# A streaming encoder's MoE layers: 16 KB read-back, zeros during the mixer, down loads on ACT's queue

## The reference

```python
def moe_layer(x, router_w, router_b, w_gate, w_up, w_down, sh_gate, sh_up, sh_down):
    ...
    _, idx = lax.top_k(masked, TOP_K)                    # 8 of 64 experts
    wts = jnp.take_along_axis(scores, idx, axis=1)
    wts = wts / jnp.sum(wts, axis=-1, keepdims=True) * ROUTED_SCALE
    routed = routed_experts(x2, idx, wts, w_gate, w_up, w_down)
    shared = (jax.nn.silu(x2 @ sh_gate) * (x2 @ sh_up)) @ sh_down
    return (routed.astype(x.dtype) + shared).reshape(B, S, D)
# routed_experts, for each block of tokens of one expert e:
        hb = jax.nn.silu(xb @ w_gate[e]) * (xb @ w_up[e])
        acc = acc.at[toks].add((hb @ w_down[e]).astype(jnp.float32) * gates[:, None])
```

## Time and profile before

| | |
|---|---|
| median of 3 runs | 1355.86 us (1353.26 to 1357.22) |
| the profiled execution, its own time | 1357.68 us |
| its span in the profile | 1355.5 us |
| PE busy | 1285.6 us (95%) |
| DVE, ACT, POOL busy | 568.3, 337.3, 270.5 us |
| moved by DMA | 445.95 MB, of them 428.13 by the hardware queue q1 |
| mean granted TensorE clock | 0.977 of full speed |

### The profile page before, as it was taken

The page is one execution under the profiler, slowest core; times in us unless marked ns, Lnnn a source line. Parts: engine busy times, 40 slices in busy tenths (PEclk is TensorE's granted clock), DMA queues, the critical chain, the costliest instruction groups (busy, mean ns, idle before and its releaser), DMA issues.

```text
span 1355.5 us, 17904 instructions
## 1 busy us (share of the span) xinstructions
PE 1285.6 (95%) x6318; PEld 648.6 (48%) x6318; DVE 568.3 (42%) x1229; ACT 337.3 (25%) x689; POOL 270.5 (20%) x233
## 2 busy tenths in 40 slices
PE   6999999999999999999989789999999999999985
PEld 4566546545444454444533565544444444444432
DVE  0665556433333343333342784332333333343336
ACT  0643412222222222222211341222222212222113
POOL 6110102122211121121202202121122211221120
PEclk9999898999999999999998889999999999999988
DMA  9403028699999999999999725999999999999992
GB/s 279 128 7 125 11 99 327 264 387 414 408 390 420 420 391 421 420 420 392 419 323 413 301 94 189 378 406 417 381 420 420 420 395 419 420 390 419 374 353 86
DMA packets 82323, 445.95 MB, mean 329 GB/s; under 512 B 20626, under 2 KB 22786, under 8 KB 32224
## 3 DMA queue, kind: packets, MB, share of 16 engines
q1 hardware_dynamic: 69248, 428.13, 79.2%
q0 software_dynamic: 13024, 17.13, 4.1%
HBM read 436.37 MB, written 35.31 MB: 348 GB/s over the span
## 4 chain that ended last, share of the span: by engine, by line
PE 88%; DMA 6%; DVE 3%; ACT 2%; issue 1%; SPq 0%; DVEq 0%
PE bank L975 32%; PE bank L894 19%; PE bank L928 15%; PE bank L922 8%; DMA sb_wslot<-in_moe_w_up_dram 4%; PE bank L878 3%; PE bank L1317 3%; PE bank L1103 1%; PE bank L1066 1%; DMA sb_wslot<-in_pool_scale_dram 1%; PE bank L987 1%; DMA sb_x<-in_x_sample_dram 1%; PE bank L1094 0%; PE bank L1234 0%; ACT sb_xt L1504 0%
## 5 line engine op out<-in xcount | busy, mean ns | idle before, releaser
L757 POOL TENSOR_TENSOR sb_sent<-sb_yh,sb_yl 128x1024 f32<-128x1024 f32 x56 | 135.5, 2420 | 651.9 <-DVE sb_yl L1729 579.0
L975 PE MATMUL bank<-sb_wslot,sb_xt 128*64 128x512 f32 x1024 | 232.1, 607 | 12.0 <-DMA sb_wslot<-in_moe_w_up_dram 12.0
L928 PE MATMUL bank<-sb_wslot,sb_ht 128*64 128x512 f32 x1024 | 231.0, 593 | 0.0
L975 PE MATMUL bank<-sb_wslot,sb_xg_own 128*64 128x512 f32 x1024 | 226.5, 595 | 1.7 <-ACT sb_xg_own L1448 1.7
L1723 DVE TENSOR_TENSOR sb_x<-sb_x,bank 128x512 f32<-128x512 f32 (+1 forms) x284 | 175.5, 680 | 80.4 <-PE bank L922 80.1
L1748 DVE TENSOR_TENSOR sb_hh<-sb_sg,bank 128x256 f32<-128x256 f32 x64 | 27.0, 421 | 399.4 <-ACT sb_sg L1473 399.4
L1729 DVE SCALAR_TENSOR_TENSOR sb_yl<-bank,sb_gslot,sb_yh 128x512 fp32r<-128x512 f32 x128 | 96.1, 750 | 160.6 <-ACT sb_yh L1455 160.6
L1473 ACT ACTIVATE sb_sg<-bank 128x256 f32<-128x256 f32 x64 | 24.6, 384 | 533.0 <-PE bank L975 533.0
L975 PEld LDWEIGHTS bank<-sb_wslot,sb_xt 128*64 128x64 f32 x1024 | 71.8, 139 | 156.0 <-issue 156.0
L894 PE MATMUL bank<-sb_pick,sb_xh 128*128 128x512 f32 x384 | 144.2, 405 | 0.0
L928 PEld LDWEIGHTS bank<-sb_wslot,sb_ht 128*64 128x64 f32 x1024 | 72.8, 137 | 144.6 <-issue 140.7
(11 more groups left out here) (325 smaller groups left out, 1149.3 us busy)
## 6 DMA issues: line engine op xcount, KB each, us to landing
sb_wslot<-in_moe_w_gate_dram SPq DMA_DIRECT2D x64, 2048.0 KB, 10.5
sb_wslot<-in_moe_w_up_dram SPq DMA_DIRECT2D x64, 2048.0 KB, 15.4
sb_wslot<-in_moe_w_down_dram SPq DMA_DIRECT2D x64, 2048.0 KB, 17.5
sb_w_in_hi<-in_w_in_dram SPq DMA_DIRECT2D x2, 2048.0 KB, 15.0
sb_w_in_lo<-in_w_out_dram SPq DMA_DIRECT2D x1, 4096.0 KB, 13.9
tail_slots<-sb_sent POOLq DMA_DIRECT2D x8, 512.0 KB, 10.8
sb_w_in_lo<-in_w_in_dram SPq DMA_DIRECT2D x2, 1024.0 KB, 11.1
sb_ln_g<-in_ln_g_dram POOLq DMA_DIRECT2D x4, 512.0 KB, 4.9
```

Source lines behind the costliest of these rows:

```text
L757: gp.tensor_tensor(sent[:, :], yh[:, :].bitcast(F32), yl[:, :].bitcast(F32), ALU.add).then_inc(s["sent_made"], 1)
L928: last = pe.matmul(y_b[c][64 * e:64 * e + 64, :], ht[:, k, 64 * e:64 * e + 64], w_down[u][:, e, k * D + c * 512:k * D + (c + 1) * 512], st ...
L975: last = pe.matmul(gu_b[64 * e:64 * e + 64, :], xgt[b][:, k, sl], w_gu[u][:, :, e, k * FE:(k + 1) * FE], start=k == 0, stop=k == DK_SLICES ...
```

## The change

Four things are done. (1) `slots_zeroed` becomes one semaphore for both layers; POOL sets `sq` to zero after the stores of ckv and krope and from it writes both layers' `tail_slots` with 16 DMAs of 128 runs of 2 KB (256 KB each), issued before it waits for `qh`. POOL's experts part waits for them before the first send, and DVE's first `square_sums` waits too. The memset of `sent` and its four DMAs behind the routing are gone. (2) The read-back takes half h of a token's eight slots (4096 values, 16 KB in one run) instead of 512 columns of all eight slots (8 runs of 2 KB). Partitions 0 to 63 then hold slots 0 to 3 and partitions 64 to 127 slots 4 to 7, all columns. Two adds of 2048 and 1024 values, a move of 64 x 1024 values and a third add of 64 x 1024 sum them. (3) SP no longer loads the down weights in its loop. ACT issues the down load of pair i + 1 in turn i, behind `high_out` of pair i - 1 (which has waited for that pair's down), and at the end of a body that of the next but one, behind the second `high_out`. The first down loads of a layer and those of further rounds stay on SP. (4) Where SP waited for `down_done` it now goes on with the next gate and up.

```diff
@@ -70,6 +70,7 @@
 DIRECT = P + WT_COLS
 TAIL_SLOTS = 64 * TOPK
 NOWHERE = 2.0 * TAIL_SLOTS
+ZERO_PARTS = DEPTH * TAIL_SLOTS * D // (P * 512)
 SLOTS = 64
 ZEROED = 13
 MIX_PARAMS = 10
@@ -556,6 +557,7 @@
         state_in = sem("state_in")
         w_out_in = sem("w_out_in")
         zeroed = sem("zeroed")
+        slots_zeroed = sem("slots_zeroed")
         wg2_zeroed = sem("wg2_zeroed")
         q_lev_zeroed = sem("q_lev_zeroed")
         k_lev_zeroed = sem("k_lev_zeroed")
@@ -599,7 +601,7 @@
             "gu_done0", "gu_done1", "down_done0", "down_done1", "xg_done0", "xg_done1", "xg_copied0", "xg_copied1",
             "pick_ready", "sg_ready", "h_ready", "ht_done", "ht_copied", "place_done", "place_copied", "gate_ready",
             "yh_ready0", "yh_ready1", "sum_done", "added", "y_half", "y_ready", "next_round",
-            "y_summed", "tail_sent", "slot_free", "sent_made", "slots_zeroed", "tail_in", "tail_step")} for l in range(DEPTH)]
+            "y_summed", "tail_sent", "slot_free", "sent_made", "tail_in", "tail_step")} for l in range(DEPTH)]
         for n in ("pool_in", "pool_c_in", "pool_scaled"):
             L[1][n] = sem(n)
 
@@ -647,27 +649,21 @@
             with sp.Fori(1, TURNS - 1) as j:
                 sp.wait_ge(s["gu_done1"], j)
                 load_pair(sp, l, 1, 2 * j + 1, GU)
-                sp.wait_ge(s["down_done0"], j)
-                load_pair(sp, l, 0, 2 * j, DN)
                 sp.wait_ge(s["gu_done0"], j + 1)
                 load_pair(sp, l, 0, 2 * j + 2, GU)
-                sp.wait_ge(s["down_done1"], j)
-                load_pair(sp, l, 1, 2 * j + 1, DN)
             sp.wait_ge(s["gu_done1"], TURNS - 1)
             load_pair(sp, l, 1, PAIRS - 1, GU)
-            for u in range(2):
-                sp.wait_ge(s[f"down_done{u}"], TURNS - 1)
-                load_pair(sp, l, u, PAIRS - 2 + u, DN)
             sp.wait_ge(s["rounds_ready"], 1)
             rounds = sp.value_load(n_rounds[0:1, 0:1], min_val=1, max_val=MAX_ROUNDS)
             with sp.If(rounds - 1):
                 with sp.Fori(1, rounds) as r:
+                    for u in range(2):
+                        sp.wait_ge(s[f"down_done{u}"], r * TURNS)
+                        load_pair(sp, l, u, u, DN)
                     with sp.Fori(0, TURNS) as j:
                         for u in range(2):
                             sp.wait_ge(s[f"gu_done{u}"], r * TURNS + j)
                             load_pair(sp, l, u, 2 * j + u, GU)
-                            sp.wait_ge(s[f"down_done{u}"], r * TURNS + j)
-                            load_pair(sp, l, u, 2 * j + u, DN)
             if l == 0:
                 uses = rounds * TURNS
                 sp.wait_ge(s["gu_done0"], uses)
@@ -743,11 +739,7 @@
             rounds = gp.value_load(n_rounds[0:1, 0:1], min_val=1, max_val=MAX_ROUNDS)
             banks.full(gp, ("lgT", l))
             gp.wait_ge(s["init"], 5 - l)
-            gp.memset(sent[:, :], 0.0).then_inc(s["sent_made"], 1)
-            gp.wait_ge(s["sent_made"], 1)
-            for k in range(TAIL_SLOTS // P):
-                gp.dma_start(slots[k * P:(k + 1) * P, :], sent[:, :]).then_inc(s["slots_zeroed"], 16)
-            gp.wait_ge(s["slots_zeroed"], 16 * (TAIL_SLOTS // P))
+            gp.wait_ge(slots_zeroed, 16 * ZERO_PARTS)
             gp.wait_ge(s["w_ready"], 2 - l)
 
             def send(r, turn, u):
@@ -755,7 +747,7 @@
                 i = r * PAIRS + turn
                 gp.wait_ge(s["y_ready"], 2 * i + 1)
                 gp.tensor_tensor(sent[:, :], yh[:, :].bitcast(F32), yl[:, :].bitcast(F32), ALU.add).then_inc(s["sent_made"], 1)
-                gp.wait_ge(s["sent_made"], r * SENT + turn + 2)
+                gp.wait_ge(s["sent_made"], r * SENT + turn + 1)
                 gp.sem_inc(s["y_summed"], 1)
                 gp.indirect_dma_start(out=slots, out_offset=bass.IndirectOffsetOnAxis(ap=slot_at[1 - u][:, 0:1], axis=0),
                                       in_=sent[:, :], in_offset=None, bounds_check=TAIL_SLOTS - 1, oob_is_err=False)\
@@ -767,17 +759,18 @@
                 with gp.Fori(0, SENT // 2) as j:
                     for u in range(2):
                         send(r, 2 * j + u, u)
-            src = slots.rearrange("(t k) d -> t k d", k=TOPK)
-            for c in range(2):
+            src = slots.rearrange("(t k) d -> t (k d)", k=TOPK)
+            for h in range(2):
                 for r0, n in ((0, TAIL), (SAMPLE_ROW, N_DEC)):
-                    gp.dma_start(xg_own[64 * c + r0:64 * c + r0 + n, :].rearrange("p (k d) -> p k d", k=TOPK),
-                                 src[r0:r0 + n, :, c * 512:(c + 1) * 512]).then_inc(s["tail_in"], 16)
+                    gp.dma_start(xg_own[64 * h + r0:64 * h + r0 + n, :], src[r0:r0 + n, h * 4096:(h + 1) * 4096]).then_inc(s["tail_in"], 16)
             gp.wait_ge(s["tail_in"], 16 * 4)
-            for i, w in enumerate((2048, 1024, 512)):
+            for i, w in enumerate((2048, 1024)):
                 gp.tensor_tensor(xg_own[:, 0:w], xg_own[:, 0:w], xg_own[:, w:2 * w], ALU.add).then_inc(s["tail_step"], 1)
                 gp.wait_ge(s["tail_step"], i + 1)
-            gp.dma_start(xg_own[0:64, 512:1024], xg_own[64:128, 0:512]).then_inc(s["tail_in"], 16)
+            gp.dma_start(xg_own[0:64, 1024:2048], xg_own[64:128, 0:1024]).then_inc(s["tail_in"], 16)
             gp.wait_ge(s["tail_in"], 16 * 5)
+            gp.tensor_tensor(xg_own[0:64, 0:1024], xg_own[0:64, 0:1024], xg_own[0:64, 1024:2048], ALU.add).then_inc(s["tail_step"], 1)
+            gp.wait_ge(s["tail_step"], 3)
             gp.wait_ge(s["added"], rounds * ROUND_ADDS + 1)
             gp.tensor_tensor(x[0:64, 2, :], x[0:64, 2, :], xg_own[0:64, 0:1024], ALU.add).then_inc(s["tail_step"], 1)
 
@@ -835,6 +828,12 @@
                 gp.dma_start(po[0:2 * P, :].rearrange("(t p) c -> p t c", p=P), src[:, 0:2, :]).then_inc(stored, 16)
                 gp.dma_start(po[2 * P:N_PROMPT, :], src[0:TAIL, 2, :]).then_inc(stored, 16)
                 gp.dma_start(so, src[SAMPLE_ROW:SAMPLE_ROW + N_DEC, 2, :]).then_inc(stored, 16)
+            gp.memset(sq[:, :], 0.0).then_inc(zeroed, 1)
+            gp.wait_ge(zeroed, ZEROED + 1)
+            for l in range(DEPTH):
+                rows = a["tail_slots"][l].rearrange("(p r) d -> p (r d)", p=P)
+                for c0 in range(0, rows.shape[1], 512):
+                    gp.dma_start(rows[:, c0:c0 + 512], sq[:, :]).then_inc(slots_zeroed, 16)
             banks.full(gp, ("qh", MH - 1))
             gp.memset(q_few_rot, 0.0).then_inc(few_zeroed, 1)
             for j in range(2):
@@ -1473,6 +1472,8 @@
                     act.activation(sg[:, :], gu_b[:, 0:FE], ACT.Silu).then_inc(s["sg_ready"], 1)
                     if m:
                         high_out(1 - u, i - 1, n - 1 + u, summed)
+                        if not last_body or m < BODY - 1:
+                            load_pair(act, l, 1 - u, BODY * j + (m + 1), DN)
                         hidden_out(i)
                     act.wait_ge(s["place_done"], i + 2)
                     nt = TILES if places_tail(m, last_body) else 2
@@ -1486,6 +1487,8 @@
                         hidden_out(i)
                     if m == BODY - 1:
                         high_out(u, i, n, summed if last_body else summed + 1)
+                        if not last_body:
+                            load_pair(act, l, u, BODY * j + (BODY + 1), DN)
 
             with act.Fori(0, rounds) as r:
                 for kk in range(DK_SLICES):
@@ -1936,6 +1939,8 @@
             turn_queries(range(4, 8))
 
             def square_sums(t):
+                if t == 0:
+                    dve.wait_ge(slots_zeroed, 16 * ZERO_PARTS)
                 for c, j in CHUNK_PARTS[4 * t:4 * t + 4]:
                     banks.copied(dve, ("o", c, j))
                 o, q = og[:, 2 * t:2 * t + 2, :, :].rearrange("p c j n -> p (c j) n"), sq[:, :].rearrange("p (i n) -> p i n", i=4)
```

## The result

The changed kernel took 1370.24 us (median of 4 runs, 1366.79 to 1373.23), the kernel before 1354.91 us beside it (1353.26 to 1357.22). The ratio is 1.0107, with a 95% interval of 1.0086 to 1.0128. It is 15 us slower, outside the predicted range of 1339 to 1364. The profiled span grew from 1355.5 to 1369.9 us, by 14.4.

What follows compares the result with a forecast made beforehand. It took TensorE, busy 95% of the span, as the bound, with DMA only 0.45 us a turn from it. Layer 1's +2.2 us and layer 0's +0.4 made +2.6 us, so 1358 us, range 1339 to 1364.

Steps and rivals of the forecast that it cites:

- The read-back's price (10 us): Tail-row read-back in 16 KB runs: costs the weight loads 10 us, not 11.7, so pair 30's load comes 1.7 us earlier.
- (a): Read-back: short runs were the cost, 16 KB runs pass at full rate, 3.7 us; 1340 us in total, chance 0.25.
- (b): Read-back: half way, a cost of 6 to 8 us; 1345 to 1352 us in total, chance 0.10.
- (c): Read-back: runs are cut into the same 4 KB packets, nothing gained; +6 us, 1362 in total, chance 0.08.
- Down loads ahead of pair 30 (+5.0 us): Last body: on its own queue a 2.1 MB down load passes before pair 30's loads are complete, +5.0 us.
- Pair 30's arrival (715.6 us): Layer 0's pair 30 up load: 713.8 - 1.7 + 5.0 - 1.5 = 715.6, so +1.8 us.
- The idle hole (-1.5 us): Body's end: ACT issues the down load near 621.5, filling 1.5 us of unused DMA time, -1.5 us.
- ACT's issue (0.35 us per turn): Last body's turns without gather: issuing down loads delays ACT 0.35 us per turn; only turn 6 counts, +0.35 us per layer.
- Zeros in the mixer: Zero writes moved from after routing into the mixer: removal worth nothing, 16 added POOL issues (9 us) hidden in idle time.
- Layer 1's mixer (-1.8 us): Mixer after layer 0: pool_scale lands earlier, LayerNorm now decides, so layer 0 costs 2.2 - 1.8 = 0.4 us.
- The sum: Whole kernel: +2.6 us on the profiled 1357.7 us, 1.8 us over the median 1355.86; predicted 1358.3, say 1358 us.
- Rival (d): Steady turns: two hardware queues in alternation carry less than one, turns slip 0.37 us at 390 GB/s; about 1370 us, chance 0.12.

Runs made afterwards that it cites:

- a2_down_sp: The changed kernel with the down loads back on SP's queue, 16 KB read-back and mixer zeros kept: 1356.34 us, ratio 0.9993 to the kernel before.
- b3_none_act: The changed kernel, down loads on ACT's queue, without the four read-back copies: 1336.39 us, ratio 0.9864 to the kernel before.
- b4_none_sp: The changed kernel with down loads back on SP's queue and without the read-back copies: 1336.15 us, ratio 0.9854 to the kernel before.
- a4_last_body_sp: The changed kernel with down loads of pairs 26 to 31 issued by SP as before, earlier ones by ACT: 1356.65 us, ratio 1.0002 to the kernel before.
- a3_zeros: The kernel before with only the zeros in the mixer added (2 KB read-back, down loads on SP): 1352.65 us, ratio 0.9974 to the kernel before.
- c1_spread_sp: The changed kernel, down loads on SP, 16 KB read-back into every second and fourth partition, four small copies after: 1344.44 us, ratio 0.9918 to the kernel before.

## Why the prediction was wrong

**The read-back's price (10 us), right alone.** I took 10 us after against 11.7 before, because the target's width and not the run's length made it. On one queue it is 11.0, and spreading the target, with the run kept, removed the stall. The rivals (a) and (b), which needed short runs to be the cost, are refuted. So is the premise of (c): the software packets fell from 448 (384 of 4 KB and 64 short ones fit the bytes) to 160, as the long runs were not cut into 4 KB.

**Down loads ahead of pair 30 (+5.0 us), right alone.** Between the issue of pair 30's up load and its matmuls 10.66 MB passed after (684.22 to 721.64) and 8.24 MB in `a2_down_sp` (686.85 to 713.70), 2.42 MB or 5.8 us more. Of the 10.66 MB the down loads' queue sent 3.54.

**Pair 30's arrival (715.6 us), the step that failed.** "713.8 - 1.7 + 5.0 - 1.5" adds a price of the read-back that stands by itself to a price of the queue that stands by itself. That is wrong, because the one changes the other. The own queue takes turns from the read-back too, so the slow stretch lasted 8 us longer. In the same two stretches 37.4 us held 25.4 us of bytes at 420 GB/s and 26.9 us held 19.6: 12.0 lost against 7.2, so +4.8 us that no term had. I had the one-to-one alternation of queues in hand and applied it to the weights alone. That `b3_none_act` and `b4_none_sp` are alike doesn't show this by itself, since by the prediction's reckoning pair 30 has 6.0 us to spare without a read-back, and 5 us of bytes ahead of it hide there; the count of bytes and the longer landings do.

**The idle hole (-1.5 us), filled but worth nothing.** ACT issues the last down load of a body at 618.80, and 624:630 moves 417 GB/s. `a4_last_body_sp` moves 425 GB/s from 626 to 632, where `a2_down_sp` moves 255, and yet waits 5.02 us for pair 30 against 5.10 (7.14 against 5.97 in layer 1), in the same total time. Why the early bytes do no good isn't shown; that a queue which waits for buffers to come free can't run ahead would explain it.

With -0.7 + 5.8 + 4.8 in place of -1.7 + 5.0 - 1.5 the wait grows by 9.9 us; it grew by 10.0 in layer 0. In layer 1 it grew by 6.8. There 10.32 MB passed after in 34.9 us (1281.14 to 1316.08) and 8.44 MB in `a2_down_sp` in 27.7 us (1274.95 to 1302.67): 4.5 us more for bytes, and 10.4 us lost against 7.6, 2.8 more. With the 0.4 us that `a2_down_sp` waits less than before, that is 6.9 with the rounding.

**ACT's issue (0.35 us per turn), too dear.** From pair 30's matmuls to pair 31's it is 14.66 us in `b3_none_act` (701.75 to 716.41) and 14.67 in `b4_none_sp` (705.75 to 720.42): nothing. After, TensorE waits 0.53 us for gslot just before pair 29's matmuls (at 689.25), as before.

**Zeros in the mixer, nothing or a little gain.** The 16 issues lie at 72.10 to 80.62, and POOL is idle for 17.53 us after them. `a3_zeros` is 0.3% faster with an interval from 0.1 to 0.4%. Its profiled span is 1.3 us shorter, of which 0.9 are there before the zeros are written, so the traces don't show where a gain would be.

**Layer 1's mixer (-1.8 us), right in number, by luck in its reason.** LayerNorm decides and 1.6 us come back. But by the prediction pool_scale lands 3.2 us earlier, and it landed 2.9 us later (12.9 us after its issue at 751.11, and 17.8 after 743.33 before). It is in time because TensorE and LayerNorm come later still. The 1.3 us of slower start were not foreseen.

**The sum.** 1355.86 + 2.6 is 1358.5 and not 1358.3, which changes nothing.

**Rival (d) gave 1370 us, the right time from a wrong mechanism.** Two hardware queues carry hardly less: turns still last 15.40 us (matmuls at 553.36, 568.75 and 584.15), and the engines move 418 GB/s from 575 to 590, where it was 421. What it had right is that a slip before pair 30 comes on top of the read-back.

## What to carry to other kernels

Before a transfer gets a queue of its own, ask what shares the DMA with it at the tightest point: a further queue takes turns from all others, and where one of them slows everything while it runs, it then runs longer. Prices of contention, each worked out alone, need not add up. And a copy of many bytes into few neighbouring partitions is better spread over all 128, even at the price of a smaller narrow copy afterwards; that was worth 10 us here (`c1_spread_sp` against `a2_down_sp`), while the length of the runs was worth nothing that could be told and the own queue cost 6 to 15 us beside every read-back tried.

## What the runs showed of the hardware

- The target's partitions set the rate of everything that runs beside a copy, not its own alone: 1.57 MB in 16 KB runs into 16 and 32 neighbouring partitions held all queues to 254 GB/s for 18 us, the same runs into every second and fourth partition to 420.
- Runs of 16 KB in place of 2 KB shortened the landing from 25.2 to 19.0 us, and gave next to nothing to the loads beside it: 11.7 and 11.0 us lost.
- An additional hardware queue with 126 MB left the rate in steady turns at 418 GB/s (421 before) and the turn at 15.40 us. With no read-back at all the time was the same within the noise (1336.39 against 1336.15 us); beside the spread one, which held 411 to 424 GB/s, it cost 6.5 us.
- A read-back of 96 runs of 16 KB passed as 160 software packets and one of 768 runs of 2 KB as 448, which fits packets of 16 KB and of 4 KB with 64 short ones in each.
